# A tuned two-block transformer kernel on one core: the products that broadcast a layer's reciprocal root move between the output tiles of its second weight unit

## What is computed

```python
def rms_norm(x, g):
    xf = x.astype(jnp.float32)
    y = xf * lax.rsqrt(jnp.mean(xf * xf, axis=-1, keepdims=True) + EPS)
    return (y * g.astype(jnp.float32)).astype(x.dtype)

    for layer in range(DEPTH):
        hn = rms_norm(h, norm_attn[layer])
        ...
        h = h + conv_ffn(rms_norm(h, norm_ffn[layer]), ffn_w_in[layer], ...)
    return rms_norm(h, final_norm)
```

## Time and profile before

| what | value |
|---|---|
| median of three runs | 2403.89 us |
| the profiled execution | 2403.94 us |
| its span | 2401.8 us |
| mean granted TensorE clock | 0.989 |
| TensorE matmul busy | 2330.0 us, 97% |
| VectorE, ScalarE, GpSimd busy | 54%, 40%, 19% |

### The profile page before, as it was taken

How to read it: one execution, slowest core, us unless ns; L and a number is a source line. 1 busy time by engine, 2 the same in 40 slices (tenths; PEclk the granted TensorE clock), 3 DMA queues, 4 the chain that set the end, 5 groups by cost and what they waited for, 6 DMA issues and landing times.

```text
span 2401.8 us, 30420 instructions
## 1 busy us (share of the span) xinstructions
PE 2330.0 (97%) x11616; PEld 1841.9 (77%) x11616; DVE 1290.7 (54%) x1690; ACT 955.6 (40%) x1401; POOL 445.1 (19%) x431
## 2 busy tenths in 40 slices
PE   9999999999998989999999999999999999999998
PEld 7775668888887658888888768888888757888887
DVE  6447646664547566665456855433346575433333
ACT  4327853443323373443333353322324762323222
POOL 0003434110004135110004034200122003311010
PEclk9999999999999999999999999999999999999999
DMA  5211002222222112222223112222222202222222
GB/s 186 105 71 36 2 3 99 92 103 89 97 96 96 53 36 88 94 99 89 103 87 132 71 53 88 91 102 105 89 104 98 86 2 87 88 105 88 104 99 77
DMA packets 31494, 203.80 MB, mean 85 GB/s; under 512 B 4260, under 2 KB 5288, under 8 KB 7720
## 3 DMA queue, kind: packets, MB, share of 16 engines
q1 hardware_dynamic: 30104, 199.37, 23.4%
q10 hardware_dynamic: 1296, 3.15, 0.4%
HBM read 200.41 MB, written 2.10 MB: 84 GB/s over the span
## 4 chain that ended last, share of the span: by engine, by line
PE 85%; DVE 7%; ACT 5%; issue 2%; POOL 1%; DMA 0%; SPq 0%; POOLq 0%; ACTq 0%; DVEq 0%
PE D L583 73%; PE X L694 3%; PE D L708 3%; PE D L716 2%; ACT prob L1325 1%; DVE w_lo L1661 1%; ACT w_hi L1121 1%; DVE xg L1695 1%; ACT prob_t L1121 1%; PE X L700 1%; PE X L819 1%; DVE prob L1994 1%; DVE mid L1690 0%; PE X L649 0%; DMA w_raw<-in_weights 0%
## 5 line engine op out<-in xcount | busy, mean ns | idle before, releaser
L583 PE MATMUL D<-xg,w_hi 128*128 128x512 f32 x3184 | 989.4, 392 | 9.6 <-DVE xg L1695 6.9
L583 PE MATMUL D<-mid,w_hi 128*128 128x512 f32 x2308 | 716.1, 392 | 15.6 <-DVE mid L1661 7.2
L583 PEld LDWEIGHTS D<-xg,w_hi 128*128 128x128 f32 x3184 | 598.3, 188 | 138.9 <-DVE xg L1695 6.6
L583 PE MATMUL D<-xg,w_lo 128*128 128x512 f32 x1592 | 621.1, 390 | 0.0
L1661 DVE TENSOR_TENSOR w_lo<-w_raw,w_hi 128x2048 fp32r<-128x2048 f32 (+2 forms) x210 | 458.0, 2182 | 289.6 <-ACT w_hi L1121 289.4
L1121 ACT ACTIVATE w_hi<-w_raw 128x2048 fp32r<-128x2048 f32 (+2 forms) x210 | 355.9, 1695 | 591.5 <-PE D L583 587.6
L583 PEld LDWEIGHTS D<-mid,w_hi 128*128 128x128 f32 x2308 | 434.7, 189 | 110.2 <-issue 12.4
L583 PE MATMUL D<-mid,w_lo 128*128 128x512 f32 x1154 | 450.7, 391 | 0.0
L583 PEld LDWEIGHTS D<-xg,w_lo 128*128 128x128 f32 x1592 | 299.8, 188 | 62.7
L1720 DVE TENSOR_TENSOR h<-D,h 128x1024 f32 (+1 forms) x71 | 86.9, 1224 | 353.5 <-PE D L583 353.4
L583 PEld LDWEIGHTS D<-mid,w_lo 128*128 128x128 f32 x1154 | 217.7, 189 | 45.6
(11 more groups left out here) (284 smaller groups left out, 1820.8 us busy)
## 6 DMA issues: line engine op xcount, KB each, us to landing
w_raw<-in_weights SPq DMA_DIRECT2D x184, 1024.0 KB, 4.8
h<-in_x SPq DMA_DIRECT2D x4, 512.0 KB, 7.5
out_y<-h SPq DMA_DIRECT2D x4, 512.0 KB, 2.9
w_raw<-in_weights SPq DMA_DIRECT2D x2, 512.0 KB, 7.0
inv_cnt<-in_inv_cnt ACTq DMA_DIRECT2D x1, 1024.0 KB, 4.8
cos<-in_cos ACTq DMA_DIRECT2D x3, 256.0 KB, 4.2
sin<-in_sin ACTq DMA_DIRECT2D x3, 256.0 KB, 5.3
vec<-in_vec SPq DMA_DIRECT2D x1, 272.0 KB, 2.8
```

What stands on the lines that cost most here:

```text
L583: last = nc.tensor.matmul(out, w[a], x[b], start=start and k == 0, stop=stop and k == 2)
```

## The change

`norm_sums` is cut in two. It keeps the sums and their signal to ScalarE. The wait for the reciprocals and the products that spread them become `spread_rstd`, which is given to the second unit's `project` as `middle` in every layer. In swa, where the swap of the first queries stood there alone, both are issued, the spreading first. The last norm calls both, one behind the other, as before. No instruction is added or removed; ScalarE's, VectorE's, GpSimd's and SyncE's programs are the same.

```diff
--- before.py
+++ after.py
@@ -644,6 +644,9 @@
                         last = nc.tensor.matmul(X[:, 3, QT + t:QT + t + 1], sq_all[:, 0, span(t)], ones_col[:, :],
                                                 start=True, stop=True)
                 last.then_inc(ms_done, 1)
+
+            def spread_rstd(norm):
+
                 pe.wait_ge(rstd_done, norm + 1)
                 for t in range(QT):
                     last = nc.tensor.matmul(X[:, 2, span(t)], rstd_t[:, t:t + 1].to_broadcast([P, P]),
@@ -667,7 +670,7 @@
                         if name == "in0":
                             project(u0, x_norm, norm=l)
                             norm_sums(l)
-                            project(u0 + 1, x_norm)
+                            project(u0 + 1, x_norm, middle=lambda: spread_rstd(l))
                             done = 2
                         with pe.Fori(0, (count - done) // 2) as i:
                             for j in range(2):
@@ -940,7 +943,7 @@
 
                 project(at["cmp_in"], x_norm, norm=l)
                 norm_sums(l)
-                project(at["cmp_in"] + 1, x_norm)
+                project(at["cmp_in"] + 1, x_norm, middle=lambda: spread_rstd(l))
                 project(at["k"], x_norm)
                 project(at["k"] + 1, x_norm, middle=lambda: swap_keys(0))
                 compressed_hidden(0, at["cmp_w1"], lambda: swap_keys(1))
@@ -970,8 +973,12 @@
             def swa(l, at):
                 q = at["q"]
                 project(q, x_norm, norm=l)
+                def spread_and_swap():
+                    spread_rstd(l)
+                    swap(q, X[:, 0:2, :])
+
                 norm_sums(l)
-                project(q + 1, x_norm, middle=query_swap(q, 0))
+                project(q + 1, x_norm, middle=spread_and_swap)
                 project(q + 2, x_norm, middle=query_swap(q + 1, 1))
                 project(at["kv"], x_kv, middle=query_swap(q + 2, 0))
                 pe.wait_ge(q_ready, qpairs_before[l] + 2)
@@ -991,7 +998,7 @@
 
                 project(at["u"], x_norm, norm=l)
                 norm_sums(l)
-                project(at["u"] + 1, x_norm)
+                project(at["u"] + 1, x_norm, middle=lambda: spread_rstd(l))
                 project(at["kv"], x_norm)
                 project(at["q"], x_norm, middle=lambda: key_swap(at["kv"], 0))
                 u = at["pool"]
@@ -1054,7 +1061,7 @@
 
                 project(at["xr"], x_norm, norm=l)
                 norm_sums(l)
-                project(at["xr"] + 1, x_norm)
+                project(at["xr"] + 1, x_norm, middle=lambda: spread_rstd(l))
                 project(at["cq"], x_norm)
                 u = at["gates0"]
                 recurrent_gates(u, 0, ((X, 0), (X, 2), (D, 2 * (u % 2)), (X, 0)))
@@ -1108,6 +1115,7 @@
                 else:
                     programs[kind](l, first[l])
             norm_sums(L_END)
+            spread_rstd(L_END)
 
 
         @block.scalar
```

## The result

The changed kernel took 2422.94 us (median of four runs, 2421.26 to 2424.22) against 2403.16 (2399.30 to 2404.64) of the kernel before: a ratio of 1.0090, with a 95% interval of 1.0078 to 1.0102. That is 19.8 us slower between the two medians; 21.6 had been forecast. (The quotient of the medians is 1.0082. The ratio on record, 1.0090, would be 21.6 us.) The execution that was profiled is the shortest of the four, 2421.26 us, with a span of 2419.1 against 2401.8, so the trace holds 17.3 us of the difference.

What follows compares the result with a forecast made beforehand. TensorE, holding 85% of the chain that ended last, was taken to bound the kernel. New waits of 15.6 us plus 6.0 for clock gave 21.6 on 2403.94: 2425.5 us, range 2416 to 2432.

Steps and rivals of the forecast that it cites:

- the mechanism: Each layer: TensorE waits where the chain from broadcast to third unit outlasts 5.45 us of cover; long waits also lose clock.
- nsa: First layer: an 11.3 us chain against 5.45 of cover makes TensorE wait 5.8 us; +5.5 us, plus 2.1 for clock.
- two ffn: Both ffn layers: the later broadcast stays hidden; 0 us in the first and -0.5 in the second.
- swa: Swap of the first queries: TensorE waits 1.8 to 1.9 us for zq, less 0.57 saved; +1.3 us.
- even: Layer with two broadcasts: most of the shift is absorbed by the attention's start; +0.3 us, bounds -1.1 and +2.
- odd: Recurrence: first gate comes late, TensorE stands some 3.6 us; +2.4 us after 2.4 of slack, plus 1.3 for clock.
- two mlp: Both mlp layers: a 9.2 us chain makes TensorE wait 3.8 us, less 0.57 saved; +3.3 us each, clock extra.
- the clock behind the mlp waits: Behind each mlp layer's new wait TensorE runs at a lower clock; 1.3 us each, lowered from 1.6.
- The cover of 5.45 against a chain of 5.0: Both ffn layers: TensorE's remaining half unit hides the third unit's low split, by only 0.45 us.
- its upper bound: Even layer: +2 us, if the low clock lasts through 1320.
- TensorE needs them at 1353.2: Even layer's pool: keys come at about 1354.8, a start 1.6 us late, taken up by the 2.52 us wait behind it.
- the list of waits that may cost the clock: New waits of 5.8 us in nsa, 3.8 in each mlp and 3.6 in odd; clock loss 6.0 us together.

Runs made afterwards that it cites:

- e9: The changed kernel once more, unaltered, on another chip: 2422.75 us against 2400.33 for the kernel before, ratio 1.0089.
- e2: The kernel before with the broadcast moved to the middle of the second unit in the two mlp layers only: 2412.00 us against 2400.90, ratio 1.0052.
- e12: The kernel before with the broadcast moved to the middle of the second unit in the odd layer only: 2407.09 us against 2400.33, ratio 1.0024.
- e8: The kernel before with the broadcast moved to the middle of the second unit in the two ffn layers only: 2400.44 us against 2400.41, ratio 1.0002.
- e5: The kernel before with the broadcast behind the first 6 matmuls of the second unit in all eight layers: 2397.81 us against 2400.41, ratio 0.9989.
- e6: The kernel before with the broadcast behind the second unit's first 6 matmuls, nsa left in the old order: 2396.17 us against 2400.41, ratio 0.9982.

## Why the prediction was right

It had said slower, 2425.5 us with a range of 2416 to 2432; it came out at 2422.94, and the mechanism is the one it gave. The parts that were timed alone, beside its terms (clock included):

| part | forecast | measured alone | by sections, all traces |
|---|---|---|---|
| nsa | 5.5 + 2.1 = 7.6 | 7.0 | 7.7 |
| two ffn | -0.5 | 0.0 | -0.5 |
| swa, even, odd | 1.3 + 0.3 + 2.4 + 1.3 = 5.3 | 3.9 | 1.1 + 2.0 + 3.5 = 6.6 |
| two mlp | 6.6 + 2.6 = 9.2 | 11.1 | 10.6 |
| all | 21.6 | 19.8, and 22.4 in e9; the parts' sum is 22.0 | about 24 |

The 19.8 and the 22.4 differ by their baselines: the changed kernel itself came to 2422.94 and 2422.75. That the forecast is within 2 us of either is partly luck: the waits were put a little too high, the clock behind the mlp waits and the even layer too low.

**nsa.** The third unit was forecast for 41.1 after a wait of 5.8; it came at 40.30 after 5.50. The whole trace stands 0.6 us earlier from its start, which is most of the difference. The prediction said nothing of what the wait's disappearance does to the second unit: it now waits 0.39 us for its own low split. Net 5.50 + 0.39 - 0.60 - 0.16 = 5.1 us; 5.5 forecast.

**The two ffn.** The cover of 5.45 against a chain of 5.0 held. VectorE's low split of the third unit in the second ffn, after:

```profile
959.46 2.29 DVE L1669 TENSOR_TENSOR w_lo<-w_raw,w_hi 128x2048 fp32r<-128x2048 f32 x1 [0.58 <-ACT w_hi L1129]
```

It ends at 961.75, 4.9 us behind the broadcast's end (955.94 + 0.91 = 956.85). TensorE never stops.

**swa.** 1.87 was forecast for the wait, 1.60 measured; the net is 1.0 instead of 1.3.

**even: here a step failed,** though its term came out no higher than its upper bound. The prediction had TensorE come to the pool's first product at 1353.2 and the keys (kd) done at 1354.8, a start 1.6 us late, which the wait for w_lo behind it would take up. The product needs the keys because it overwrites the bank X that their rotation reads; in the program TensorE waits for k_ready there. TensorE and VectorE after:

```profile
1354.82 2.78 DVE L2084 TENSOR_TENSOR kd<-rope_t 64x512 f32<-64x512 f32 x4
...
1357.82 0.70 PE L583 MATMUL X<-mid,w_hi 128*128 128x512 f32 x2 [3.50 <-issue]
```

The bracket names nothing, but the row starts 0.2 us behind the end of kd (1354.82 + 2.78 = 1357.60) on VectorE, and TensorE's last product ahead of it starts at 1353.93. Set back by the 2.9 us that the trace stands late at this layer's start, that is a keys' end of 1354.7, right as forecast, and TensorE ready at 1351.4 rather than 1353.2. The failed step is the sentence "TensorE needs them at 1353.2". That is about when TensorE got there in the old order (1353.33 in the trace before); in the new order it got there 1.9 us earlier, without the 1.31 us wait and with a half-clock stretch of 3.4 us behind the sums instead of 6.8. So the wait is 3.50 instead of 1.6. It does swallow the 2.52 us behind it, as was said. But a wait of that length was left out of the list of waits that may cost the clock, and the clock fell here, to 0.50 from 1358.8. The attention came at 1376.49, 1.96 later than before when the 2.9 are taken off; 0.3 had been forecast, with 2 as its bound. The section itself varies, 0.05 to 2.79 in the five traces with the change; its mean is 2.0 above the five traces without it, at the prediction's upper bound and not at its 0.3.

**mlp.** A wait of 3.8 was forecast, 3.56 and 3.55 measured; the net of 3.3 measured 3.17 where the clock stayed. The term that was mis-sized is the clock behind it: 1.3 us taken for each, whereas six unfilled mlp sections (after, e9, e2) lost 2.85, 2.75, 1.57, 2.69, 0 and 2.76, 2.1 in the mean. The prediction had lowered a loss of 1.6, read off behind the wait of 2.74; the rows with 2.1 and 2.6 would have been the better neighbours. "Since one may miss it" was right for one of the six.

**odd.** 3.6 forecast for the wait, 3.47 measured. TensorE's wait is right. For the layer 2.4 + 1.3 = 3.7 was forecast and the sections give 3.5, though the timing of e12 gave 6.8.

**The two sums.** By the pages, TensorE stood 13.3 us longer in the changed kernel and 13.7 in e9 (busy 2337.5 of a span of 2423.0), against 15.6 forecast. Adding up the rows above gives 5.1 - 0.6 + 1.0 + 1.0 + 3.0 + 3.0 + 2.3 = 14.8, where even is 3.50 and a new wait of 1.36 for q_even less the old 1.31 and 2.52, and odd 3.47 less two of 0.57. Another 1.2 went in the waits for xg (6.9 before, 5.7 after): one of 1.15 in the first layer's first unit, where nothing had been changed, is missing after. The running got longer by 4.0 us, in e9 by 7.5, against 6.0 forecast. So the waits were put a little high, and the clock came out near its term by some luck: five waits lost clock rather than four, 2.9 us at worst, but in single traces up to half of it was missing elsewhere, because falls that the kernel before has at other places (10.2 us at 190.3, 3.4 at 1903.8) were shorter or absent. The prediction's evidence for a wait without a fall, 2.52 us in even, was chance as well: the same wait was followed by a fall in three of the seven traces that have it (e8, e5, e6).

**The rule that was weighed.** The Trainium skill, "TensorE: Matmul & The Clock Gate", Part 1, puts the ramp penalty under 1% of a typical kernel's span and says not to fit a particular count of slow matmuls. The prediction read it more widely, as a reason to leave the clock out. What this change added is inside the one per cent: 4 to 7.5 us of 2420 are 0.2 to 0.3%. The share of the clock not granted over the whole span is a little outside it, 1.1% in the trace before (0.989) and 1.2 to 1.4% in the two of the changed kernel (0.988, 0.986), some of it while TensorE stood. For an edit whose whole effect is 20 us it is a fifth to a third of it, and leaving it out would have given 2419.5, which is below all timings of the changed kernel.

## What to carry to other kernels

Before hiding a wait of the bounding engine behind more of its own work, follow what the delayed result feeds: on each in-order queue, everything written behind its first user is delayed too, next weights included, and the work moved ahead of the producer is taken away as cover behind it, so the same 24 matmuls count twice. Move by little more than the wait is long: here 6 matmuls, 1.36 us, hid 0.57 us and gained 4.2 us where the chain left room (some of it from clock falls that went away), and 24 hid the same and lost 20. And give a new wait of 3.5 us or more on TensorE something on top for its clock: here 2.1 us in the mean of six, 2.9 at most.

## What the hardware showed that was not expected

The same wait, 3.56 and 3.55 us in front of the same code, left the granted clock at 1.00 once and took it to 0.51 the other time, in one execution (e2). The wait of 2.74 us for mla_qr, behind which the kernel before had a fall, had none in the changed kernel:

```profile
1916.72 0.73 PE L583 MATMUL D<-mid,w_hi 128*128 128x512 f32 x2 [2.74 <-ACT mla_qr L1129]
```

The two matmuls took 0.73 us here and 1.22 before. Counted over all fourteen traces, the clock fell in this wait (2.7 to 2.8 us) or within 1.6 us behind it in 7 of 14 cases, with the 2.5 us in even in 3 of 7, with the new 3.5 to 3.6 us in 17 of 18, and with those of 5.2 to 5.5 us in 32 of 32. So the longer the wait, the surer the fall, and in this kernel it came nearly every time from 3.5 us on.

Falls also come and go in stretches whose code, and whose waits nearby, are unchanged; single sections moved by up to 3.3 us and the first 24 us by 2 us with them. In a comparison of two traces this is the largest noise of this kernel, many times the repeatability of the second ffn's section and of an unchanged mlp's (0.1 us). What spared the one wait of 3.56 us, and what decides it for the waits of 2.5 to 2.8 us, was not settled.
